# Entry of an up-projection in a hybrid decoder layer: order of the last transposes, of the operand combinations and of the second pair's weight sums, and the start address of the shared on-chip region

## The reference

```python
hn = rms_norm(h, ffn_norm_w[l])
up = causal_depthwise_conv(hn @ w_up[l], ffn_conv_w[l], ffn_conv_b[l])   # (1024, 1024) @ (1024, 5632), conv width 3
a, gt = jnp.split(up, 2, axis=-1)
h = h + (jax.nn.silu(gt) * a) @ w_down[l]
```

## Time and profile before

| | |
|---|---|
| median of 3 runs | 1985.4 us (1983.98 to 1985.51) |
| the profiled execution | 1986.32 us, its span 1984.5 us |
| mean granted TensorE clock | 0.991 of full |
| PE busy | 1939.7 us (98% of the span), 9113 matmuls |
| DVE busy | 1098.7 us (55%) |
| ACT busy | 738.3 us (37%) |
| stages with the change | w_out to 1292.7 us, up 1292.87 to about 1739, down to the end |

### The profile page before, as it was taken

How to read it: one execution, slowest core, us unless ns; L and a number is a source line. 1 busy time by engine, 2 the same in 40 slices (tenths; PEclk the granted TensorE clock), 3 DMA queues, 4 the chain that set the end, 5 groups by cost and what they waited for, 6 DMA issues and landing times. The chain is left out here.

```text
span 1984.5 us, 24170 instructions
## 1 busy us (share of the span) xinstructions
PE 1939.7 (98%) x9113; PEld 1652.3 (83%) x9113; DVE 1098.7 (55%) x1413; ACT 738.3 (37%) x1324; POOL 99.1 (5%) x153
## 2 busy tenths in 40 slices
PE   6999999999999999999999999989999999999999
PEld 5788999999998887887887887768888888778887
DVE  5535532443351876896415535477878787743433
ACT  6323532432252155223523332454545454432222
POOL 1101110111010010000000010000000000000000
PEclk9999999999999998999999999989999999999999
DMA  6211221021113101102113404202222222264312
GB/s 243 96 43 43 71 70 43 12 80 48 43 65 107 43 1 43 43 22 64 43 43 101 135 22 170 96 11 96 77 82 84 74 90 69 72 245 149 111 48 74
DMA packets 112412, 152.33 MB, mean 77 GB/s; under 512 B 13705, under 2 KB 60809, under 8 KB 112329
## 3 DMA queue, kind: packets, MB, share of 16 engines
q1 hardware_dynamic: 104265, 140.60, 21.4%
q10 hardware_dynamic: 8064, 10.59, 1.4%
HBM read 122.73 MB, written 28.43 MB: 76 GB/s over the span
## 5 line engine op out<-in xcount | busy, mean ns | idle before, releaser
L241 PE MATMUL psum<-whi,act_lo 128*128 128x512 f32 x768 | 314.7, 410 | 3.0 <-DVE act_lo L1432 2.4
L243 PE MATMUL psum<-whi,act_hi 128*128 128x512 f32 x768 | 304.9, 397 | 0.0
L242 PE MATMUL psum<-wlo,act_hi 128*128 128x512 f32 x768 | 304.2, 396 | 0.0
L241 PEld LDWEIGHTS psum<-whi,act_lo 128*128 128x128 f32 x768 | 195.1, 254 | 18.2 <-issue 4.0
L243 PEld LDWEIGHTS psum<-whi,act_hi 128*128 128x128 f32 x768 | 195.1, 254 | 15.4
L242 PEld LDWEIGHTS psum<-wlo,act_hi 128*128 128x128 f32 x768 | 195.6, 255 | 13.0
L241 PE MATMUL psum<-act_hi,wlo 128*128 128x512 f32 x512 | 203.7, 398 | 0.0
L243 PE MATMUL psum<-act_hi,whi 128*128 128x512 f32 x512 | 200.6, 392 | 0.0
L242 PE MATMUL psum<-act_lo,whi 128*128 128x512 f32 x512 | 200.4, 391 | 0.0
L194 ACT CAST whi<-stage 128x512 fp32r<-128x512 f32 x200 | 120.1, 621 | 183.6 <-PE psum L243 175.6
L199 DVE TENSOR_TENSOR wlo<-stage,whi 128x512 fp32r<-128x512 f32 x200 | 129.0, 685 | 95.1 <-ACT whi L194 94.2
(11 more groups left out here) (248 smaller groups left out, 3591.1 us busy)
## 6 DMA issues: line engine op xcount, KB each, us to landing
stage<-in_w_in SPq DMA_DIRECT2D x144, 256.0 KB, 4.1
u_raw<-in_w_up SPq DMA_DIRECT2D x44, 512.0 KB, 4.6
gated_scratch<-g_buf SPq DMA_DIRECT2D x22, 512.0 KB, 2.6
gated<-gated_scratch SPq DMA_DIRECT2D x22, 512.0 KB, 3.4
d_stage<-in_w_down SPq DMA_DIRECT2D x44, 256.0 KB, 2.9
group_out<-ob ACTq DMA_DIRECT2D x24, 256.0 KB, 2.1
grp<-group_out SPq DMA_DIRECT2D x24, 256.0 KB, 3.1
stage<-in_w_mem_kv SPq DMA_DIRECT2D x16, 256.0 KB, 7.9
```

The source lines that it names most:

```text
L241: nc.tensor.matmul(dst, lhs[1], rhs[0], start=first, stop=False, skip_group_check=True)
L242: nc.tensor.matmul(dst, lhs[0], rhs[1], start=False, stop=False, skip_group_check=True)
L243: return nc.tensor.matmul(dst, lhs[0], rhs[0], start=False, stop=last, skip_group_check=True)
```

## The change

It does four things.

1. Statistics are packed more tightly, and `FREE` is rounded up to a multiple of 512 from `bottom`. The shared region begins at byte 134272, 128 bytes lower, 128 past a multiple of 512, like the low region. Everything placed relative to `FREE` moves with it.
2. PE makes the last transposes before product 1 of pair 1. DVE and ACT evacuate them earlier, and the combinations (4, 0) and (4, 1) move to the end, on DVE after `h_dve_lo` of parts 4 and 5. The low halves get an order of their own, `T_LOWS`.
3. The weight sums of pair 1 are made in the output stage, two after each of DVE's steps 8 and 9, in place of the first pair's `pair_dve`.
4. `u_next` moves from behind `u_sums` into the buffer `u_raw[0]`. So the casts into it wait for all of pair 0's low halves, and the load of pair 2 into the same buffer waits for products 1 and 2 of pair 1.

```diff
-        STATS = SMALL + 1024 + (NVECS * 4 + 63) // 64 * 64
+        STATS = SMALL + 1024 + (NVECS * 4 + 31) // 32 * 32
...
-        row_scale = at("row_scale", STATS + 544, [NT + MT])
-        FREE = (STATS + 544 + 64 + P - 1) // P * P
+        row_stats = at("row_stats", STATS + 416, [3, NT + MT])
+        row_sumsq, row_meansq, row_scale = (row_stats[:, i, :] for i in range(3))
+        FREE = (STATS + 536 + 511) // 512 * 512
...
-        u_next = [at("u_next_hi", U_W + 45056, [2, HALF_K, P], F32R),
-                  at("u_next_lo", U_W + 45056 + 4096, [2, HALF_K, P], F32R)]
+        u_next = [at("u_next_hi", U_W, [2, HALF_K, P], F32R), at("u_next_lo", U_W + 4096, [2, HALF_K, P], F32R)]
...
-        T_SUMS = [(i, q) for q in range(2) for i in (1, 2, 3, 4)]
-        T_HALVES = [(2, 0), (3, 0), (1, 0), (4, 0), (2, 1), (3, 1), (1, 1), (4, 1)]
+        T_SUMS = [(1, 0), (2, 0), (3, 0), (1, 1), (2, 1), (3, 1), (4, 0), (4, 1)]
+        T_HALVES = [(2, 0), (3, 0), (1, 0), (2, 1), (3, 1), (1, 1), (4, 0), (4, 1)]
+        T_LOWS = [(2, 0), (3, 0), (2, 1), (3, 1), (1, 0), (1, 1), (4, 0), (4, 1)]
...
+            if isinstance(U, int) and U == 2:        # up_load
+                for i in (1, 2):
+                    sp.wait_ge(up_p[i], 2)
...
             if ahead:                                # up_act_hi
-                for n in S_OF:
+                for n in range(1, 8):
                     act.wait_ge(up_lo[n], 1)
...
                     elif step in (NT, NT + 1):       # w_out_stage, first_pairs
                         up_dve_lo(dve, 1, 1, step - NT + 1, True)
+                        for s in (0, 1) if step == NT else (2, 3):
+                            up_dve_sum(dve, 1, 0, 1, s)
...
                 t_dve_sum(dve, 3, 0)                 # end of w_out_stage, vector
-                t_dve_sum(dve, 4, 0)
...
                 up_pe_2(pe, 0, 0)                    # up_stage, tensor
-                pe.wait_ge(row_ss, hr.tile0 + NT)
-                up_pe_1(pe, 1, 1, True)
                 pe.wait_ge(row_scaled, hr.tile0 + NT)
                 pe.wait_ge(h_raw, 3 * KT)
                 for k in range(KT):
                     h_last_pe(pe, k)
+                pe.wait_ge(row_ss, hr.tile0 + NT)
+                up_pe_1(pe, 1, 1, True)
                 up_pe_2(pe, 1, 1, True)
...
-                if not last:                         # pair_dve, twice
+                if not last and not start:
                     for n in range(3):
                         up_dve_sum(dve, U + 1, half_next, np, n)
```

More of the change, by code:

```diff
@@ L158, in build @@
         ln_sums = at("ln_sums", STATS + 384, [6])
-        row_sumsq = at("row_sumsq", STATS + 416, [NT + MT])
-        row_meansq = at("row_meansq", STATS + 480, [NT + MT])
-        row_scale = at("row_scale", STATS + 544, [NT + MT])
-        FREE = (STATS + 544 + 64 + P - 1) // P * P
+        row_stats = at("row_stats", STATS + 416, [3, NT + MT])
+        row_sumsq, row_meansq, row_scale = (row_stats[:, i, :] for i in range(3))
+        FREE = (STATS + 536 + 511) // 512 * 512
         psum = ctx.enter_context(nc.psum_tensor("psum", [P, 8, CW], F32))
@@ L1817, in up_dve_sum @@
                 dve.wait_ge(raw_loaded[par], 32 * half_U + 32)
-                if isinstance(U, int) and U == 1:
-                    dve.wait_ge(up_p[1], 2)
-                    dve.wait_ge(up_p[2], 2)
                 ins = nc.vector.tensor_tensor(u_sums[:, 0], value_low, up_block(par, 4), ALU.add)
@@ L2140, in tensor @@
                     h_last_pe(pe, k)
+                pe.wait_ge(row_ss, hr.tile0 + NT)
+                up_pe_1(pe, 1, 1, True)
                 up_pe_2(pe, 1, 1, True)
-                pe.wait_ge(t_lo, T_HALVES.index((2, 1)) + 1)
+                pe.wait_ge(t_lo, T_LOWS.index((2, 1)) + 1)
                 up_pe_6(pe, 0, 0)
-                pe.wait_ge(t_lo, T_HALVES.index((3, 1)) + 1)
+                pe.wait_ge(t_lo, T_LOWS.index((3, 1)) + 1)
                 up_pe_7(pe, 0, 0)
-                pe.wait_ge(t_lo, T_HALVES.index((1, 1)) + 1)
+                pe.wait_ge(t_lo, T_LOWS.index((1, 1)) + 1)
                 up_pe_5(pe, 0, 0)
@@ L2149, in tensor @@
                 up_pe_3(pe, 0, 0)
-                pe.wait_ge(t_lo, T_HALVES.index((4, 1)) + 1)
+                pe.wait_ge(t_lo, T_LOWS.index((4, 1)) + 1)
                 up_pe_4(pe, 0, 0)
@@ L2193, in scalar @@
             def scalar(act):
-                t_act_hi(act, T_HALVES[1:4])
                 for k in (0, 1, 4, 5):
                     h_last_act(act, k)
+                t_act_hi(act, T_HALVES[1:3])
                 up_s1(act, 0, 0)
-                t_act_hi(act, T_HALVES[4:7])
+                t_act_hi(act, T_HALVES[3:6])
                 h_act_hi(act, [5])
-                t_act_hi(act, T_HALVES[7:8])
+                t_act_hi(act, T_HALVES[6:8])
                 for U in range(3):
@@ L2221, in pair_dve @@
                     up_dve_lo(dve, U, par, 3)
-                if not last:
+                if not last and not start:
                     up_dve_sum(dve, U + 1, half_next, np, 3)
@@ L2244, in vector @@
             def vector(dve):
-                t_dve_lo(dve, T_HALVES[0:1])
-                h_dve_lo(dve, [4])
-                t_dve_lo(dve, T_HALVES[1:4])
                 for k in (2, 3, 6, 7):
@@ L2251, in vector @@
                 t_dve_sum(dve, 2, 1)
-                t_dve_lo(dve, T_HALVES[4:5])
+                t_dve_lo(dve, T_HALVES[0:1])
                 t_dve_sum(dve, 3, 1)
-                t_dve_lo(dve, T_HALVES[5:7])
-                h_dve_lo(dve, [5])
+                t_dve_lo(dve, T_HALVES[1:2])
+                t_dve_lo(dve, T_HALVES[3:5])
+                t_dve_lo(dve, T_HALVES[2:3])
+                t_dve_lo(dve, T_HALVES[5:6])
+                h_dve_lo(dve, [4, 5])
+                t_dve_sum(dve, 4, 0)
                 t_dve_sum(dve, 4, 1)
-                t_dve_lo(dve, T_HALVES[7:8])
+                t_dve_lo(dve, T_HALVES[6:8])
+                dve.wait_ge(t_lo, len(T_LOWS))
                 for U in range(3):
```

## The result

| | before | changed |
|---|---|---|
| median | 1985.45 us (1983.98 to 1987.75, 4 runs) | 1972.36 us (1969.47 to 1973.54, 4 runs) |
| ratio, 95% interval | | 0.9931 [0.9914, 0.9948] |
| profiled execution, its span | 1986.32, 1984.5 us | 1971.36, 1969.6 us |
| PE busy | 1939.7 us | 1918.9 us |

What follows compares the result with a forecast made beforehand. PE, busy 98% of the span, bounds the kernel; at the entry, DVE then ACT's copy. Address 16.8 plus entry 3.0 makes 19.8 us off 1985.4 (the median): 1966 us forecast, range 1962.5 to 1982.5.

Steps and rivals of the forecast that it cites:

- The rival (0.20): Matmuls across both regions: low versus high address costs, not the remainder, so moving 128 bytes changes nothing; 1982.4 us, chance 0.20.
- the term of 16.8 us: Address saving by matching remainders: up stage 12.6 us, branch inputs 3.9, memory stage 0.3, all on PE's path.
- the 3.9 of the branch inputs: Branch inputs in three stages: 576 matmuls, each 6.7 ns faster, save 3.9 us.
- the main case's own range: Whole kernel, address and entry gains both working: 1966 us, between 1962.5 and 1970; chance 0.77.
- the second case: Whole kernel: the address has no effect and only the entry gains; 1982.4 us, between 1980.6 and 1985.4, chance 0.20.
- the lowest value for the address, 14: Whole kernel: at worst the address saves 14 us, added to 1.5 for the entry.
- gain of 3.0 us: Up-stage entry: 4.2 us from earlier products less 1.2 for the clock, bounds 0 and 4.8.
- the 1.2 us set down for the clock: Entry: half of some 2.6 us, since a clock fall in either idle stretch seemed equally likely.
- "lost openly" case: Entry: the clock falls in the second idle stretch, products 5 and 3 run slow, some 2.6 us are lost.
- The second term: Entry, product 5 to product 3: early sums let casts follow the first copy, 3.7 us instead of 4.53, another 0.8 gained.
- The hidden items: Pair 2's load lands by 1310.6 us, sums of 2.8 us fit DVE's 4.15 idle, casts into `u_next` cost nothing.
- Late loads: Shared-region weight loads off multiples of 256 take over 13.5 us, so pairs wait; 1996 us, chance 0.03.

Runs made afterwards that it cites:

- Region only: Kernel before with only the shared region moved from 256 to 128 past a multiple of 512 (tighter statistics, new `FREE`): 1973.79 us against 1985.21, ratio 0.9947.
- both regions at 256: Kernel before with the low region moved up 128 bytes, shared one left in place, so both are 256 past a multiple of 512: 1973.18 us, ratio 0.9941.
- Entry only: Changed kernel with the shared region put back to 256 past a multiple of 512: 1982.75 us against 1985.21, ratio 0.9989.

## Why the prediction was right, and where it was off

**Right: the address.** The surcharge belonged to the difference of the operands' remainders, read from the fast pair in the earlier trace rows beside the earlier trace rows. Region only and both regions at 256 show it. The rival (0.20) falls with the first, since a move by 128 bytes was to change nothing; the second adds that an operand which did not move became fast. The Trainium skill's rule in "TensorE: Matmul & The Clock Gate", "Step-by-step: what each phase is for", that the two read ports do not take from each other, has no room, as the prediction read it, for what the traces show: 233.4 ns against 226.7 for the same matmul. Whether it is the ports that collide, no run shows; the runs give the condition, not the circuit behind it. Two details were wrong or too simple: I took remainders at 512, it is 256; and equal differences need not cost the same (229.1 ns for the branch inputs at 64 bytes).

**Too high: the term of 16.8 us.** Alone it measured 11.4 by the medians, 12.0 and 13.4 in the two other kernels that remove the surcharge, and 13.1 between the changed kernel's profiled execution and that of the kernel before, outside the entry. The surcharge per matmul was a little over-read: from pair 1's product 6 to the end of the up stage PE is busy for 11.4 us less over 1740 matmuls, 6.6 ns each and not 6.8. More was lost by the sentence "all of it on PE's path". The entry's 108 products save 0.7 us into a wait. In the branch and output stages PE waits longer for DVE now. The three largest waits of PE for DVE from 827 to 1292 us (engine line waited for: us in total, times, longest), before and then changed:

```profile
PE psum L241 <- DVE act_lo L1432: 2.4, 2, 1.6
PE psum L241 <- DVE wlo L199: 1.9, 1, 1.9
PE psum L1405 <- DVE grp L1370: 1.2, 1, 1.2
```
```profile
PE psum L240 <- DVE act_lo L1431: 2.9, 2, 2.1
PE psum L240 <- DVE wlo L198: 2.1, 1, 2.1
PE psum L1404 <- DVE grp L1369: 1.9, 2, 1.0
```

5.5 us have become 6.9, so 1.4 of the 3.9 of the branch inputs were given back. (The third of them varies by itself: it is 0.8 in region only.) At the first product of the down stage it is 0.8 more: 1.32 us of waiting for DVE's low half of the weights, 0.49 before. Its row in the changed kernel:

```profile
1724.64 0.50 PE L240 MATMUL psum<-d_hi,gs_lo 128*128 128x512 f32 x1 [1.32 <-DVE d_lo L2103]
```

Together that is 1.4 + 0.8 + 0.7 = 2.9 us hidden behind DVE, and some 0.4 of over-read distance (0.25 ns over 1740 matmuls), of the 3.7 us by which 13.1 falls short of 16.8. The other 0.4 is not accounted for. That region only stood lower still is in part the fall of the clock shown there, 1.5 us in its profiled execution.

**Luck in the range.** The median of 1972.4 us lies 2.4 above the main case's own range, which ended at 1970. It is inside the stated range only because that was stretched to 1982.5 for the second case, and that case did not occur. The direction and the mechanisms were right; the bounds of the sum were too narrow, since the lowest value for the address, 14, was not low enough.

**The entry: mechanism right, gain of 3.0 us too high.** Product 6 was to wait about 2.5 us (2.63), product 5 about 4 (3.80) behind ACT's copy, product 5 to start 25.2 us after the first up matmul (25.3), DVE's subtraction (4, 1) to follow seven operations behind low (2, 1): all as worked out. The profiled execution gained 1.8 us from the first up matmul to pair 1's product 6. Entry only gained 2.5 there and 2.5 by the medians; that the two agree is in part chance, as said above. The term that failed is the 1.2 us set down for the clock: in the changed kernel's execution the fall came in the open and made product 5 to product 3 take 6.2 us where 3.7 were reckoned, 2.5 us, the "lost openly" case and not the mean of the two. The second term, 0.8 us for the early sums, was worth nothing beside the half clock under product 5, which gave DVE time for the late ones. The hidden items (load of pair 2, sums in the output stage, casts into `u_next`) showed no new wait.

Late loads, the rival on the slow side, did not occur. A load of weights takes a little longer to land, to be read beside the earlier trace rows:

```profile
u_raw<-in_w_up SPq DMA_DIRECT2D x44, 512.0 KB, 5.0
```

It is 4.6 or 4.7 us in the three kernels whose shared region begins at a multiple of 256 bytes (before, entry only, both regions at 256) and 5.0 or 5.1 in the nine others. So the start address does cost the load something, 0.4 us and not the 2.3 of the prediction's estimate, and 13.5 us are to be had the earlier trace rows.

## What to carry to other kernels

When matmul starts in one stage stand a few nanoseconds further apart than in another, compare where the two operands begin within 256 bytes before looking at anything else; giving all regions the same remainder is a change of one line, and the up stage, where PE hardly waits, kept 10.4 of 11.4 us. A stage's saving counts only up to the next wait for another engine, so subtract the waits that stand at its ends. Of a wait at a stage's entry, look at what stands ahead of the releasing instruction on its own engine: the copy behind two casts cost more here than the whole rest of the entry's reordering gained.

## What the runs showed of the hardware that was not expected

- A 128x512 fp32 matmul whose stationary and moving operands start at different remainders at 256 bytes takes 233.3 to 233.4 ns from start to start (232.4 in entry only's up stage), and 226.7 with equal ones; 32, 64 and 128 bytes of difference cost the same in the up stage, 256 nothing. With the moving operand 64 bytes past the stationary one's remainder it took 229.1 ns (the branch inputs of that run).
- A load of 512 KB into this memory landed in 4.6 to 4.7 us (median of 44) where its target began at a multiple of 256 bytes, and in 5.0 to 5.1 where it did not.
- The granted clock fell after 2.5 us of idleness in one execution (entry only) and not after 2.6 us in another of the same order (the changed kernel); what it costs depends on whether a wait follows that covers it. In a third place, behind waits of 2.09 and 0.81 us at 1200 us, it fell in region only and not in the changed kernel.
